# A full product table in place of row gathers: one half of a retrieval layer moved to TensorE

## The reference

```python
def eval_chunk(args):                       # 128 tokens at a time
    hx, e, g = args                         # tokens, 128 expert numbers and 128 gates per token
    a = jnp.einsum('cd,ckd->ck', hx, u_tab[e])
    return jnp.einsum('ck,ckd->cd', g * jax.nn.gelu(a), v_tab[e])
```

## Time and profile before

| what | us |
|---|---|
| median of 3 runs | 3481.06 (3479.72 to 3483.58) |
| span of the profiled execution, first to last instruction | 3478.2 |
| TensorE busy | 3001.3 |
| VectorE busy | 2638.9 |
| POOL busy | 2085.2 |
| ScalarE busy | 958.6 |
| DMA, mean over the span | 374 GB/s |

### The profile page before, as it was taken

The page is one execution under the profiler, slowest core; times in us unless marked ns, Lnnn a source line. Parts: engine busy times, 40 slices in busy tenths (PEclk is TensorE's granted clock), DMA queues, the critical chain, the costliest instruction groups (busy, mean ns, idle before and its releaser), DMA issues.

```text
span 3478.2 us, 36816 instructions
## 1 busy us (share of the span) xinstructions
PE 3001.3 (86%) x11060; PEld 1923.4 (55%) x11060; DVE 2638.9 (76%) x6261; ACT 958.6 (28%) x2019; POOL 2085.2 (60%) x2114
## 2 busy tenths in 40 slices
PE   8999899889998799788998689889998877777775
PEld 7788766456775556446766356445775532223222
DVE  6576698889857888888768898888757998845445
ACT  3341243333312233233212233333211232211111
POOL 1010375676656766766566675666556777777774
PEclk9999999989999989999999899999999999999998
DMA  5335699999999999999999999999999999999997
GB/s 179 121 122 206 255 409 409 408 403 385 409 409 409 404 398 409 409 407 386 404 408 409 409 388 409 409 409 380 409 409 409 409 407 409 409 405 388 409 409 306
DMA packets 361796, 1299.19 MB, mean 374 GB/s; under 512 B 40257, under 2 KB 44737, under 8 KB 361473
## 3 DMA queue, kind: packets, MB, share of 16 engines
q0 software_dynamic: 298960, 1087.79, 79.1%
q1 hardware_dynamic: 62640, 209.06, 15.7%
HBM read 1282.01 MB, written 14.68 MB: 373 GB/s over the span
## 4 chain that ended last, share of the span: by engine, by line
PE 37%; DMA 30%; DVE 12%; POOL 12%; issue 7%; ACT 1%; DVEq 0%; ACTq 0%; POOLq 0%
DMA heap<-table_v,heap 27%; PE ps L977 17%; POOL heap L935 12%; PE ps L1207 11%; DVE heap L2165 4%; PE ps L1144 4%; DMA heap<-table_u,heap 3%; DVE heap L1861 1%; PE ps L1037 1%; PE ps L1128 1%; PE ps L1106 1%; PE ps L1088 1%; PE ps L1018 0%; PE ps L1094 0%; ACT heap L1485 0%
## 5 line engine op out<-in xcount | busy, mean ns | idle before, releaser
L1207 PE MATMUL ps<-heap 128*128 128x512 f32 x2816 | 1436.8, 637 | 423.7 <-DMA heap<-table_v,heap 312.2
L2165 DVE CUSTOM_DVE_ANT_0 heap<-heap,ps 128x1024 f32<-128x1024 f32 x1008 | 1216.3, 1214 | 226.8 <-DMA heap<-table_u,heap 223.5
L935 POOL DMA_INDIRECT heap<-table_v,heap x1024 | 1028.7, 1005 | 581.5 <-PE ps L1207 333.1
L935 POOL DMA_INDIRECT heap<-table_u,heap x1024 | 1021.4, 997 | 485.3 <-issue 240.9
L1207 PEld LDWEIGHTS ps<-heap 128*128 128x128 f32 x2816 | 517.5, 198 | 1130.0 <-issue 841.0
L977 PE MATMUL ps<-hT,ring 128*128 128x256 f32 x3840 | 874.1, 382 | 11.1 <-DVE hT L1980 6.0
L977 PEld LDWEIGHTS ps<-hT,ring 128*128 128x128 f32 x3840 | 734.5, 192 | 174.5 <-issue 75.0
L1861 DVE SCALAR_TENSOR_TENSOR heap<-heap 128x1024 f32<-128x1024 f32 x313 | 401.6, 1283 | 273.4 <-issue 188.5
L1485 ACT ACTIVATE heap<-ident,heap 128x128 f32<-128x128 f32 x704 | 266.7, 395 | 536.1 <-PE ps L1207 320.1
L1505 ACT ACTIVATE heap<-heap 128x8 f32<-128x8 f32 x128 | 26.7, 209 | 555.5 <-DVE heap L2165 555.3
L1144 PE MATMUL ps<-temp,ring 128*128 128x256 f32 x640 | 150.5, 384 | 1.5 <-ACT temp L1359 1.0
(11 more groups left out here) (270 smaller groups left out, 2583.4 us busy)
## 6 DMA issues: line engine op xcount, KB each, us to landing
ring<-weights SPq DMA_DIRECT2D x344, 512.0 KB, 7.3
ring<-ssm_par SPq DMA_DIRECT2D x36, 512.0 KB, 8.9
heap<-table_u,heap POOLq DMA_INDIRECT x1024, 12.7
heap<-table_v,heap POOLq DMA_INDIRECT x1024, 12.6
ssm_par<-heap POOLq DMA_DIRECT2D x20, 512.0 KB, 4.9
ring<-weights SPq DMA_DIRECT2D x20, 256.0 KB, 6.3
ssm_par<-heap POOLq DMA_DIRECT2D x8, 256.0 KB, 3.0
xT<-x_cm SPq DMA_DIRECT2D x2, 512.0 KB, 4.7
```

The lines of the kernel that those rows point to most:

```text
L935: pool.indirect_dma_start(rows[:, j, :], None, table, bass.IndirectOffsetOnAxis(expert[:, tile % 2, k:k + 1], 0)).then_inc(landed, 16)
L1207: mm = pe.matmul(ps[:, SUM_BANK + half, :], diag[:, PE_TURN[v] % DIAGS, :], rows_v[:, v % NV, half * 512:(half + 1) * 512], start=(k == 0) ...
L2165: dve.tensor_tensor_reduce(row, row, token, 1.0, 0.0, ALU.mult, ALU.add, act_st[:, g % 3, pick % GROUP:pick % GROUP + 1]).then_inc(dotted, 1)
```

## The change

All tokens of a stage are multiplied with all 16384 rows of u. A host-side array `swept_u` holds the table transposed, in pieces like those of `v`. After `score`, TensorE runs 64 units `("sweep", u, n)`; each takes two pieces, covers 256 experts for both tiles and ends in one bank. ScalarE copies the bank to `swept` (which lies in the buffers `rows_u`) and, after every four units, issues two stores of 512 KB to the DRAM arrays `products`, one per tile. `product_at` holds for each pick the address of its product (token x 16384 + expert). In `GATHERS`, "u" becomes "a": POOL fetches, once the whole stage is stored, 128 single words per pick into `act_st`. `dot` is left for stages that aren't swept, and there are none. `htok` and `hload` go, `TOKEN_BANK` joins the banks of the units (six from stage 1 on), and the plan's costs and its rule for where a sum goes are changed. `squares` of the next stage waits for the last sweep unit.

```diff
+SWEPT = 4
+SWEPT_TILES = 2 * SWEPT
+DOT0 = SWEPT_TILES * PICKS
+SWEEP = 256
+SWEEPS = EXPERTS // SWEEP
+STORED = 4
+PITCH = EXPERTS
+LANDS = 4
@@ query_order
-    return out + [("htok", u, 1, 0), ("htok", u, 1, 1)]
+    return out + ([("sweep", u, n) for n in range(SWEEPS)] if u < SWEPT else [("htok", u, 1, 0), ("htok", u, 1, 1)])
@@ banks
-EARLY = UNIT[("mean", 0, 1)]
-BANK = [n % (8 if n < EARLY else 4) for n in range(len(RING_UNITS))]
+EARLY = UNIT[("mean", 1, 0)]
+LATE = len(RING_UNITS)
+BANK = [n % 8 if n < EARLY else (0, 1, 2, 3, 6, 7)[n % 6] if n < LATE else n % 4 for n in range(len(RING_UNITS))]
@@ make_plan
 SLOT_US = 2.6
+GATHER_US = 2.25
+SWEEP_SHARE = 0.75
+PE_SHARE = 0.55
...
+        if u < DOT0:
+            there, after = (("sweep", u // PICKS // 2, SWEEPS - 1), 1), LANDED
...
+            if v < DOT0:
+                slot["v_on"] = "DVE" if 0 < v % PICKS < PICKS - 1 and tile_open and waiting < 3.0 and dve_over < 1.0 else "PE"
...
+            length = GATHER_US if swept else SLOT_US
+            pe = length - (1.05 if on_pe else 0.0) - pe_over
+            dve = length - (1.35 if slot["u"] is not None and u >= DOT0 else 0.0) - (1.33 if on_dve else 0.0) - dve_over
...
-            cost = weight_of(item, 0)[1]
+            cost = weight_of(item, 0)[1] * (PE_SHARE if busy else 1.0) * (SWEEP_SHARE if item[0] == "sweep" and busy else 1.0)
@@ run_sp
+                elif name[0] == "sweep":
+                    sp.dma_start(ring[:, c % RING, :], swept_u[bass.ts(layer * SWEEP_PIECES + name[1], P), :]).then_inc(w_landed[c % RING], 16)
@@ run_pool
+                if table == "a":
+                    if pick % (2 * PICKS) == 0:
+                        for i in range(2):
+                            pool.wait_ge(sweep_stored[i], 32 * (SWEEPS // STORED // 2) * (tile // 2 + 1))
+                    if k == 0 and tile >= 2:
+                        pool.wait_ge(gelued, PICKS // GROUP * (tile - 1))
+                    if k % GROUP == 0 and g >= LANDS:
+                        pool.wait_ge(gelued, g - LANDS + 1)
+                    pool.indirect_dma_start(act_st[:, tile % 2, k:k + 1], None, products[tile][:, :],
+                                            bass.IndirectOffsetOnAxis(product_at[:, tile % 2, k:k + 1], 0)).then_inc(a_landed[g % LANDS], 16)
@@ run_pe
+                elif kind == "sweep":
+                    names = pieces_of(item)
+                    for t in range(2):
+                        for k in range(KD):
+                            mm = pe.matmul(ps[:, b, t * SWEEP:(t + 1) * SWEEP], hT[:, k, t * P:(t + 1) * P],
+                                           piece(u, names[k // 4], (k % 4) * SWEEP, SWEEP), start=(k == 0), stop=(k == KD - 1))
...
@@ run_act
+                elif kind == "sweep":
+                    b, n = done_unit(item), item[2]
+                    j = (SWEEPS * u + n) // STORED
+                    if n % STORED == 0 and j >= 2:
+                        act.wait_ge(sweep_stored[j % 2], 32 * (j // 2))
+                    at = n % STORED * SWEEP
+                    act.copy(swept[:, j % 2, :, at:at + SWEEP], ps[:, b, :].rearrange("p (t e) -> p t e", t=2)).then_inc(sweep_copied, 1)
+                    act.wait_ge(sweep_copied, SWEEPS * u + n + 1)
+                    act.sem_inc(bank_free[b], 1)
+                    if n % STORED == STORED - 1:
+                        at = n // STORED * STORED * SWEEP
+                        for t in range(2):
+                            act.dma_start(products[2 * u + t][:, :].rearrange("(p e) o -> p (e o)", p=P)[:, at:at + STORED * SWEEP],
+                                          swept[:, j % 2, t, :]).then_inc(sweep_stored[j % 2], 16)
...
+                    if g < DOT0:
+                        act.wait_ge(a_landed[n % LANDS], 16 * GROUP * (n // LANDS + 1))
@@ run_dve, settle
+                if tile < SWEPT_TILES:
+                    if tile >= 2:
+                        dve.wait_ge(gelued, (PICKS * (tile - 2) + TOPK * (h + 1)) // GROUP)
+                    ts.step(dve.tensor_scalar(product_at[:, tile % 2, cols], expert_f[:, cols], row_at[:, 0:1], None, ALU.add))
...
@@ run_dve
-                    dot(slot["u"])
+                    if slot["u"] >= DOT0:
+                        dot(slot["u"])
```

More of the change, by code:

```diff
@@ L180 @@
 RINGED = ("masks", "mean", "ssm_u", "ssm_x", "ssm_y", "q", "k", "v", "att_s", "att_p", "att_o", "pool_u", "mix", "glu_gate", "glu_val",
-          "branch", "gate", "out", "wq", "score", "htok", "tb", "wt")
+          "branch", "gate", "out", "wq", "score", "htok", "tb", "wt", "sweep")
 def weight_of(item, part):
@@ L214, in prior @@
     if kind == "final":
-        return [end("htok", STAGES - 1, 1, 1)] + ([end("final", u - 1)] if u else [])
+        return [end("sweep", STAGES - 1, SWEEPS - 1)] + ([end("final", u - 1)] if u else [])
     if kind == "mean":
@@ L368, in pieces_of @@
         return [("gate", 2 * item[2] + i, item[3]) for i in range(2)]
-    if kind == "wq":
-        return [("wq", 2 * item[2] + i) for i in range(2)]
+    if kind in ("wq", "sweep"):
+        return [(kind, 2 * item[2] + i) for i in range(2)]
     return []
@@ L414, in make_plan @@
     end_of = {}
+    used_at = {}
     shut = []
-    tokens = 0
+    tokens = SWEPT_TILES
     finals = deque(range(len(FINALS)))
@@ L448, in read_before @@
         pick = PICKS * (item[1] - 2) + TOPK * item[2] + TOPK - 1
-        return end_of.get(pick, s) + 4 < s
+        return used_at.get(pick, s) < s
     def run(eng, budget, s, out):
@@ L528, in make_plan @@
                 at, left = at + 1, None
+        if busy and swept:
+            dve += max(0.0, moved - GATHER_US)
         run("ACT", act, s, slot["ACT"])
@@ L554, in gather_order @@
         if slot["u"] is not None:
-            out.append((s, "u", slot["u"]))
+            out.append((s, "a" if slot["u"] < DOT0 else "u", slot["u"]))
         if slot["v"] is not None:
@@ L568, with trunk @@
 DVE_OF_TILE = [[v for v in ON_DVE if v // PICKS == tile] for tile in range(TILES)]
-def trunk(nc, x_cm, positions, inv_freq, weights, keys, vecs, log_dt, ssm_bc, pool_edge, table_u, table_v, final_g, out_cm):
+def trunk(nc, x_cm, positions, inv_freq, weights, keys, vecs, log_dt, ssm_bc, pool_edge, table_u, table_v, swept_u, final_g, out_cm):
     par = nc.dram_tensor("ssm_par", (DEPTH * len(PARS) * P, BLK), F32)
+    products = [nc.dram_tensor(f"products{tile}", (P * PITCH, 1), F32) for tile in range(SWEPT_TILES)]
     with ExitStack() as ctx:
@@ L771, in trunk @@
         v_free = [sem(f"v_free{j}") for j in range(NV)]
+        a_landed = [sem(f"a_landed{j}") for j in range(LANDS)]
+        sweep_copied = sem("sweep_copied")
+        sweep_stored = [sem(f"sweep_stored{i}") for i in range(2)]
         dotted = sem("dotted")
@@ L938, in run_pool @@
             for table, pick in GATHERS:
[L939 to L945, removed]
+                tile, k, g = pick // PICKS, pick % PICKS, pick // GROUP
+                if table != "v" and pick % TOPK == 0:
+                    pool.wait_ge(picks_ready, pick // TOPK + 1)
+                if table == "a":
[8 more added lines that the diff above has]
+                                            bass.IndirectOffsetOnAxis(product_at[:, tile % 2, k:k + 1], 0)).then_inc(a_landed[g % LANDS], 16)
+                elif table == "u":
+                    n = pick - DOT0
+                    if n >= NU:
+                        pool.wait_ge(dotted, n - NU + 1)
+                    gather(table_u, rows_u, n % NU, pick, u_landed[n % NU])
                 else:
+                    j = pick % NV
                     if pick >= NV:
```

98 lines of the change are left out of this document (57 added, 41 removed).

## The result

| | before | after |
|---|---|---|
| median of the runs | 3482.3 us (4 runs) | 4562.9 us (4551.0 to 4576.6, 4 runs) |
| ratio | | 1.3105, 95% interval 1.3079 to 1.3132 |
| span of the profiled execution | 3478.2 | 4549.1 |

A forecast was written before the change was run, and what follows sets the result against it. It took DMA bytes to bound the middle and tail, with POOL and TensorE close beneath. TensorE's path 3768, store and first fetch 10, tail 635 and end 25 sum to 4438, so 4440 us, range 4200 to 4740.

The forecast's parts named there:

- Sweep: On TensorE, 8192 matmul instructions over four stages at 0.2158 us each: 1768 us, 442 us a stage.
- TensorE's path to the end of sweep 3: TensorE's program order sets the time up to there: 27 + 1565 + 1768 + 258 + 150 = 3768 us.
- Picks on TensorE: Some 150 of the 768 picks of tiles 0 to 5 stay summed on TensorE, 1.72 us each: 258 us.
- Idle: TensorE idles 27 us in the first 388 us and 50 us in each of three later windows, 150 us.
- Windows: Three windows bound by TensorE, 401 + 442 + 86 + 50 = 979 us each, with POOL's 635 us fitting inside.
- Tail: After the last sweep, tiles 6 and 7 run with nothing hiding them: 256 pairs at 2.48 us, 635 us.
- Price of a fetch: A four-byte indirect fetch costs POOL 1.24 us, like a row gather, so a pair costs 2.48 us; 0.83 kept as alternative.
- (b): A fetch costs POOL less than a row gather: at 0.83 us the whole takes 4335 us; chance 0.10.
- (c): A fetch of 128 scattered words is dear for the DMA queue, say 4 us a pair: 4830 us; chance 0.05.
- Rival (a): The plan's slots, not TensorE, bound the windows: 56 picks run with TensorE idle, 139 us each, 4710 us; chance 0.17.
- Rival (d): The sweep's instructions stream faster than 0.2158 us; at 0.108 the whole would be 3560 us; chance 0.01.
- The 1313 us of DMA that are saved are worth 0.08 us a pair: Dropping the u row gathers gains little: DMA allows 2.56 us a pair and POOL stands right beneath at 2.48.

The follow-up runs named there:

- the kernel with free products: Changed kernel without sweep units, their loads and stores; words fetched from the u table, picks wait for their lists alone: 3473.8 us, 0.9963 of the kernel before.

## Why the prediction was right

By its own steps:

- *Sweep*: 8192 x 0.2158 = 1768 us; measured 1773.5. Starts at 440, ends at 882 us, first fetch at 891.8 (885 forecast). Half the loads changed nothing, half the matmuls took 810 us out of the sweeps.
- *TensorE's path to the end of sweep 3*: 3768 forecast, 3796 measured. Three terms were off and nearly cancel; that only 28 us remain is luck. Picks on TensorE: 150 (258 us) forecast, 75 ahead of the tail, 147 us busy, so 111 us too many. Idle: 177 forecast (27 + 150), measured 3796 - (3581.2 - 35.6) = 250, 73 us too few. The trunk's own work came to some 1625 in place of 1565 us, 60 too few; in the stretches of stages 1 to 3 the granted clock was 0.89 to 0.94.
- *Windows*: 979 us forecast, 949, 992 and 973 measured. Half the fetches took 46 us from them, so POOL has a small part; the forecast had it fully hidden.
- *Tail*: here is the miss. 256 x 2.48 = 635 us were forecast, and a pair took 2.80, 717 us; that is 82 of the 111 us between 4438 and 4549; the other 28 are TensorE's path. The step was "a pair costs 2.48 us": it took POOL's 0.94 us from a stretch in which hardly a sum ran on VectorE, though the change moves nearly all sums there. The rows had it already: 1.44 us for one of three gathers, 1.98 for the longest, and in the row shown above 1.005 us as the mean over the kernel before, against 0.938 in its tail. That tail was full of dot products, which leave POOL alone. With the sums on TensorE the step is right to 0.02 us.
- *Price of a fetch*: 1.24 us as for a gather: 0.944 + 0.30 in the run with the tail's sums on TensorE. Rivals (b) and (c) fall.
- *Rival (a)*: in part. Before stage 2, TensorE stood 48 us for the last picks of tile 1, before stage 3 15 us; not 139. All its idle time in the three windows is 49, 101 and 68 us, where 50 each were forecast. The wait before stage 2:

```profile
1830.79 0.59 PE L1207 MATMUL ps<-ring,hT 128*128 128x256 f32 x2
1879.20 3.75 PE L1268 MATMUL ps<-heap 128*128 128x512 f32 x4 [47.81 <-DMA heap<-table_v,heap]
```

- *Rival (d)*: 8192 instructions in 1773.5 us are 0.2165 us each; it falls.
- "The 1313 us of DMA that are saved are worth 0.08 us a pair": in the middle this was too harsh for bytes alone (140 us for 403 MB), but right for the change as it is planned: 3474 us with all products free. Its sums on VectorE raise POOL's floor as the bytes fall; that this is what holds the middle is not shown, since with fewer of them it stayed as slow.

What stays open: where the 0.3 us of issue between two POOL gathers go, since no run takes them away; which read of the gather waits for the sum; and whether another order of work could bring the middle of the kernel with free products under 3.0 us a pair.

## What to carry to other kernels

Before you take work from the engine that is full, price the next floor: here the bytes allowed 2.56 us a pair and POOL 2.48, so in the tail, a rewrite that removes 537 MB from under the bytes could at best gain 3%. Test such a rewrite with its costly new part left out altogether; that run (0.4% faster) says more about it than the full one. And take an instruction's price from a stretch in which its neighbours do what they will do after the change: not only how busy they are counts, but where their operands lie.

## What the runs showed of the hardware

- An indirect DMA of 128 indices holds POOL 0.94 us whether it fetches 4 KB, 1 KB or 4 bytes per index, and the next starts 0.30 us later.
- It takes 1.25 us on average when it starts during a 1.28 us VectorE sum with two SBUF operands; up to 2.0 us in single cases. One that starts more than 0.1 us into the sum and over 0.15 us before its end is over 0.81 to 0.82 us after the sum (183 of 183 in the tail); one that starts in the first 0.1 us takes 0.94 us, and the sum is the longer one (10 of 10).
- A VectorE instruction of 1.22 us with one operand in SBUF and one in PSUM does not touch it: 671 gathers started during one, the longest took 0.949 us.
- A float32 matmul call of 256 columns is two instructions of 0.216 us each at full clock, unbroken over 2048 of them, with 128-column weight loads of 0.19 us beneath.
- TensorE, all but idle in the tail of the kernel after (36 of 753 us busy), was granted 0.52 of its clock; with the tail's sums on it (431 of 550 us busy) it was granted 1.00.
